# The delta rule's inverse in 32x32 blocks on four strips of partitions, with a step's tail spread over the next step

## The chip, the cores and the metric

One core of one Trainium2 chip runs the whole kernel. The metric is the time of one execution in microseconds (us). The core has TensorE (PE: matrix products into PSUM, with PEld as its weight loads), VectorE (DVE), ScalarE (ACT), GpSimd (POOL) and the DMA queues, of which SyncE (SP) issues most. The engines run side by side, each through its own instructions in order, and wait for each other by semaphores.

## The reference

Two transformer-like blocks run after each other. The change touches one piece of the second: the gated delta rule of its even mixer, run forwards and backwards over 512 + 256 tokens with 8 heads of 64.

```python
m = jnp.where(strict, einsum('bhncd,bhnsd->bhncs', kb, kc) * decay, 0.0)
tmat = triangular_solve(m + eye, eye, left_side=True, lower=True, unit_diagonal=True)
u = einsum('bhncs,bhnsv->bhncv', tmat, vb)
w = einsum('bhncs,bhnsk->bhnck', tmat, kb * exp(gc)[..., None])
qk = einsum('bhncd,bhnsd->bhncs', qc, kc) * decay
def step(s, inp):
    v_new = u_i - einsum('bhck,bhkv->bhcv', w_i, s)
    o_i = einsum('bhck,bhkv->bhcv', qd_i, s) + einsum('bhcs,bhsv->bhcv', qk_i, v_new)
    s = s * gl_i[..., None, None] + einsum('bhck,bhcv->bhkv', kd_i, v_new)
```

`tmat` is the inverse of a unit triangular matrix. It is what the change computes in another way.

## The kernel before

The kernel works in fp32 and in chunks of 128 tokens, so there are 6 token tiles and 2 directions: 12 steps. `order` lists them as (direction, tile), the directions taking turns. In step n all 8 heads lie side by side along the columns of a tile.

A step goes like this. `act_rows` fetches the rows of cumulated gates by a DMA on ACT's queue. `dve_dif` takes differences and clamps them, `act_decays` turns them into decays `DU` and `DD`. `pe_kq` makes the products of keys with keys (which = 0) and keys with queries (which = 1), and `dve_kq` with `dve_kq_rest` multiplies the first into `DU` (the matrix M) and the second into `DD`. `pool_blocks` copies the two 64x64 diagonal blocks of M (8 heads) into `MC`, on partitions 0 to 63 and 64 to 127.

The inverse of these blocks is built by doubling. `XC` holds the inverse so far, `XTC` its transpose. `dve_first` sets the first level (pairs of rows), `pe_xt` transposes it on PE, `act_xt` copies that out. Then come levels 1 to 5. In each, `pool_level` masks out of `MC` the off-diagonal part `Cc` of that level, and `pe_level` computes v = Cc' XTC (16 matmuls of 64x64), which ACT copies to `VC` in two halves (`act_level`), and then z (32 matmuls), which DVE subtracts from `XTC` and `XC`, again in halves (`dve_level`). The last level joins 32x32 blocks to 64x64. Below these two blocks lies one 64x64 corner: `pe_cross`, a copy by ACT, `pe_corner`, a negated copy by DVE (`dve_corner`). `pool_gdn` copies the diagonal blocks into the full 128x128 transposed inverse `XT`.

`pe_state` applies the running state `S` to keys and queries, `pe_u` applies `XT` to the values less the state's part, `pe_s` updates the state, and `pe_o` makes the output. Of step n - 1, `pe_u`, `pe_o` and `pe_s` stand in step n, after its levels 1 and 2. `pe_side` puts other work into the loop: a chunk of a modulation product with 4 MB of weights (line 583) in steps 1, 3, 5, 7 and 9, and its fold (line 569) a step later.

The order on each engine is written out by hand in `pe_gdn`, `act_gdn`, `dve_gdn` and `pool_gdn`. PSUM has 8 banks, given out in turn by `K.open`: a matmul into a bank waits until the reader of its last content is through. Names in rows: `psum` is any bank; `feat`, `weights`, `rows` and `arena` are large tiles in which `XC`, `XTC`, `VC`, `MC`, `XT` and `DU` are columns. The level matmuls are line 2392, cross 2422, corner 2431, kq 2384, state 2444, u 2456, o 2464, s 2473. Short names such as v, z, kq, u in the text are these blocks.

## Time and profile before

| what | us |
|---|---|
| three runs | 3333.03, 3338.39, 3343.77 |
| median | 3338.39 |
| span of the profiled execution | 3342.8 |
| delta rule's loop of 12 steps (1396.3 to 1756.0) | 359.7 |
| its tail (1756.0 to 1768.4) | 12.4 |

The profile gives for the profiled execution its span, from first to last instruction, and no time of its own beside that; it lies among the three runs. PE is busy 94% of the span, DVE 50%, ACT 36%, POOL 9%. A group's row gives line, engine, operation, names and shapes, then how often, busy time, mean length in ns and the idle time ahead of it with what ended it. One fp32 matmul of the program stands as two records in the trace, each with its weight load. In a timeline, records of one kind that follow each other are one row.

### The profile page before, as it was taken

How to read it: one execution, taken by the hardware profiler on the slowest of the kernel's cores; microseconds unless marked ns; L12 is line 12 of the kernel's file. 1: busy time of each engine (PE TensorE's matmuls, PEld its weight loads, DVE VectorE, ACT ScalarE, POOL GpSimd, SP SyncE). 2: the span in 40 equal slices, each digit the busy share in tenths (PEclk: the TensorE clock that was granted, in tenths of full speed). 3: DMA queues.
4: the chain of work that ended last, by engine and by line, in shares of the span. 5: the costliest groups of instructions: out<-in, count | busy, mean ns of one | idle time of the engine just before them, and what ended most of it. 6: DMA issues, size and time to landing. Idle time of an engine off the chain costs nothing.

```text
span 3342.8 us, 55088 instructions
## 1 busy us (share of the span) xinstructions
PE 3137.0 (94%) x23594; PEld 2546.5 (76%) x23594; DVE 1659.0 (50%) x2675; ACT 1194.1 (36%) x2162; POOL 308.1 (9%) x312
## 2 busy tenths in 40 slices
PE   7989998999998999899998899999999988989998
PEld 5767887757776787788885578888888776678886
DVE  3255445344525546776765555333344456653444
ACT  4315335355531554422224444111112425642221
POOL 1020020000002100143431000000000101000000
PEclk9999999989999999999998999999999999999999
DMA  5293212260227331132211003212121324032231
GB/s 212 76 328 104 101 59 101 101 252 26 88 96 265 90 105 54 54 121 72 82 60 42 26 14 81 71 51 76 51 76 51 100 51 76 4 99 78 99 114 64
DMA packets 176062, 306.58 MB, mean 92 GB/s; under 512 B 20326, under 2 KB 41639, under 8 KB 175561
## 3 DMA queue, kind: packets, MB, share of 16 engines
q1 hardware_dynamic: 148064, 278.71, 24.9%
q0 software_dynamic: 3712, 12.74, 1.3%
q10 hardware_dynamic: 24041, 11.60, 1.3%
q8 instruction: 186, 3.05, 0.4%
q14 instruction: 59, 0.48, 0.1%
HBM read 294.87 MB, written 6.80 MB: 90 GB/s over the span
## 4 chain that ended last, share of the span: by engine, by line
PE 71%; DVE 16%; ACT 8%; DMA 2%; issue 1%; POOL 1%; ACTq 0%; DVEq 0%; SPq 0%
PE psum L425 17%; PE psum L426 17%; PE psum L427 17%; PE psum L2392 5%; PE psum L958 3%; PE psum L583 2%; ACT feat L692 2%; PE psum L977 2%; DVE small L1122 2%; DVE weights_r L369 2%; DVE arena L875 1%; DVE x_lat L878 1%; PE psum L992 1%; PE psum L2384 1%; PE psum L2456 1%
## 5 line engine op out<-in xcount | busy, mean ns | idle before, releaser
L369 DVE TENSOR_TENSOR weights_r<-weights,weights_r 128x2048 fp32r<-128x2048 f32 (+2 forms) x168 | 361.5, 2172 | 506.6 <-ACT weights_r L360 506.5
L425 PE MATMUL psum<-feat_r,weights_r 128*128 128x512 f32 (+1 forms) x1552 | 544.2, 351 | 8.5 <-DVE feat_r L722 4.9
L426 PE MATMUL psum<-feat_r,weights_r 128*128 128x512 f32 (+1 forms) x1552 | 541.9, 349 | 0.0
L427 PE MATMUL psum<-feat_r,weights_r 128*128 128x512 f32 (+1 forms) x1552 | 541.1, 349 | 0.0
L425 PE MATMUL psum<-weights_r,feat_r 128*128 128x512 f32 (+2 forms) x1344 | 527.1, 392 | 14.6 <-DVE weights_r L369 10.1
L360 ACT ACTIVATE weights_r<-weights 128x2048 fp32r<-128x2048 f32 (+2 forms) x168 | 303.1, 1825 | 634.4 <-DMA weights<-in_w_ffn_gate 208.2
L427 PE MATMUL psum<-weights_r,feat_r 128*128 128x512 f32 (+2 forms) x1344 | 520.3, 387 | 0.0
L426 PE MATMUL psum<-weights_r,feat_r 128*128 128x512 f32 (+2 forms) x1344 | 520.1, 387 | 0.0
L425 PEld LDWEIGHTS psum<-feat_r,weights_r 128*128 128x128 f32 x1552 | 295.0, 190 | 54.8 <-issue 6.2
L426 PEld LDWEIGHTS psum<-feat_r,weights_r 128*128 128x128 f32 x1552 | 295.1, 190 | 37.6
L427 PEld LDWEIGHTS psum<-feat_r,weights_r 128*128 128x128 f32 x1552 | 294.7, 190 | 37.9
L425 PEld LDWEIGHTS psum<-weights_r,feat_r 128*128 128x128 f32 x1344 | 255.7, 190 | 66.8 <-DVE weights_r L369 10.3
L427 PEld LDWEIGHTS psum<-weights_r,feat_r 128*128 128x128 f32 x1344 | 255.2, 190 | 50.3
L426 PEld LDWEIGHTS psum<-weights_r,feat_r 128*128 128x128 f32 x1344 | 255.8, 190 | 47.9
L425 PE MATMUL psum<-weights_r,arena_r 128*128 128x512 f32 x440 | 172.5, 392 | 5.7 <-DVE arena_r L521 2.8
L426 PE MATMUL psum<-weights_r,arena_r 128*128 128x512 f32 x440 | 171.4, 389 | 0.0
L427 PE MATMUL psum<-weights_r,arena_r 128*128 128x512 f32 x440 | 171.2, 389 | 0.0
L1122 DVE TENSOR_REDUCE small<-psum 128x1 f32<-128x768 f32 (+4 forms) x176 | 121.7, 691 | 42.4 <-PE psum L958 31.0
L700 POOL CAST feat_r<-feat 128x512 fp32r<-128x512 f32 x76 | 51.0, 671 | 864.6 <-ACT feat L692 864.4
L1057 ACT ACTIVATE feat<-psum,small 128x768 f32<-128x768 f32 (+2 forms) x112 | 87.3, 779 | 106.3 <-DVE small L1122 98.8
L977 PE MATMUL psum<-const,feat 128*128 128x128 f32 x544 | 84.3, 286 | 35.6 <-DVE arena L1131 16.7
L692 ACT ACTIVATE feat<-psum,small 128x128 f32<-128x128 f32 x304 | 109.4, 481 | 6.4 <-PE psum L661 6.4
(478 smaller groups left out, 4411.2 us busy)
## 6 DMA issues: line engine op xcount, KB each, us to landing
weights<-in_w_mod SPq DMA_DIRECT2D x48, 2048.0 KB, 13.0
weights<-in_gla_w_in SPq DMA_DIRECT2D x24, 1024.0 KB, 7.3
weights<-in_w_ffn_gate SPq DMA_DIRECT2D x20, 1024.0 KB, 7.6
weights<-in_w_ffn_up SPq DMA_DIRECT2D x20, 1024.0 KB, 5.1
weights<-in_w_ffn_down SPq DMA_DIRECT2D x20, 1024.0 KB, 6.3
weights<-in_fox_w_in SPq DMA_DIRECT2D x16, 1024.0 KB, 6.2
weights<-in_sgu_w_in SPq DMA_DIRECT2D x12, 1024.0 KB, 6.7
weights<-in_gla_w_out SPq DMA_DIRECT2D x8, 1024.0 KB, 6.9
```

The lines of the kernel that those rows point to most:

```text
L360: act.e.activation(WEI_r[:, s * SLOT + HALF:s * SLOT + HALF + n], WEI_t[:, s * SLOT:s * SLOT + n], ACT.Copy).then_inc(*A.put(("weights", c ...
L369: dve.e.tensor_tensor(WEI_r[:, s * SLOT:s * SLOT + n], WEI_t[:, s * SLOT:s * SLOT + n], WEI_r[:, s * SLOT + HALF:s * SLOT + HALF + n].bitc ...
L425: pe.e.matmul(ps, lh, rh, start=first, stop=False)
L426: pe.e.matmul(ps, lh, rl, start=False, stop=False)
L427: done = pe.e.matmul(ps, ll, rh, start=False, stop=last)
L583: done = pe.e.matmul(ps[32 * j:32 * j + 32, :], cond_at(mod, k, b), where[k][0], start=b == 0 and k < 4, stop=b == 1 and k >= 4)
L692: act.e.activation(FL_plain[:, k, t * P:(t + 1) * P], K.at[at][:, m * P:(m + 1) * P], ACT.Identity, bias=PRE_B[:, c0 + k:c0 + k + 1], scal ...
L958: done = pe.e.matmul(ps[m][:, n0:n0 + w], lt, rh, start=first, stop=last)
L977: done = pe.e.transpose(ps[:, c0:c0 + P], PR[n % 3][:, j * P:(j + 1) * P], ident)
L1057: act.e.activation(PR[i][:, 0:nk], src, ACT.Exp, bias=NEGM[:, i:i + 1], accum_out=SUM[:, n % 8:n % 8 + 1]).then_inc(*A.put((tag, "exp", n) ...
L1122: dve.e.tensor_reduce(NEGM[:, i:i + 1], src, AX.X, ALU.max, negate=True).then_inc(*V.put((tag, "max", n)))
L2392: done = pe.e.matmul(out_[rows, (h - heads[0]) * 64:(h - heads[0] + 1) * 64], lhsT[rows, h, :], rhs[rows] if len(rhs.shape) == 2 else rhs[ ...
```

## The change

The inverse by doubling now works on 32x32 diagonal blocks only: four of them per head, one on each strip of 32 partitions (`STRIPS`), so that a head takes 32 columns instead of 64. `XX` holds the transpose and the inverse side by side, `Cc`, `VC` and `MC` have half their columns. There are four levels instead of five. A level has 32 matmuls of 32x32 in v and 64 in z. z's two products of a half go into one bank, and DVE subtracts both in one instruction.

The fifth level becomes a join: `pe_join_v` takes the off-diagonal 32x32 blocks straight from M, ACT copies, `pe_join_z` gives the blocks for `XT` and for `XN` (the inverse of one half, needed by corner), and ACT copies them out negated, in three pieces. The corner's copy moves from DVE to ACT. `pe_xt` and `act_xt` are gone; DVE transposes 32x32 blocks itself in `dve_first`.

The join, cross, corner, u, s and o of step n - 1 are dealt out one by one between the v and z blocks of step n. So are both kq products; the one for queries moves to the end of its own step. `DU` gets a third buffer, since M is needed longer, and its rows are fetched earlier in the step; the semaphore of that DMA becomes two. The decays: DVE clamps only `DD`, in one instruction that also adds a mask of -1e30 (`NEG`), and ACT clamps `DU` by a Relu ahead of its exponential, in an own place. Key products, beta and decay are multiplied in one pass of eight 128x128 instructions (`dve_kk`). POOL copies four blocks, masks three or four levels of half the width, and assembles `XT` and `XN` in six copies (`pool_assemble`). The constant tile grows by 192 columns, and POOL makes the 32-wide identity `IDENT_S` by four small copies ahead of the mixer.

```diff
+    def pe_strips(pe, out_, lhsT, rhs, name=None):
+        for h in range(4):
+            for rows in STRIPS:
+                done = pe.e.matmul(out_[rows, h * 32:(h + 1) * 32], lhsT[rows, h, :], rhs[rows, h, :], start=True, stop=True)
+        if name is not None:
+            done.then_inc(*B.put(name))
+    def pe_v(pe, n, level):
+        C = b2(h8(Cc[level % 2]))
         for hb in range(2):
             at = (D_, "v", n, level, hb)
             ps = K.open(pe, at)
             pe.wait_ge(*G.of((D_, "C", n, level)))
-            pe.wait_ge(*(A if level == 1 else V).of((D_, "x level", n, level - 1, hb)))
-            pe_blocks(pe, ps, h8(C), h8(Xt), range(4 * hb, 4 * hb + 4), at)
+            pe.wait_ge(*V.of((D_, "x level", n, level - 1, hb)))
+            pe_strips(pe, ps, C[:, hb], XX[n % 2][:, 0, 4 * hb:4 * hb + 4, :], at)
+    def pe_z(pe, n, level):
         for hb in range(2):
+            at, v, x = (D_, "z", n, level, hb), b2(h8(VC))[:, hb], XX[n % 2][:, 1, 4 * hb:4 * hb + 4, :]
+            ps = K.open(pe, at)
             pe.wait_ge(*A.of((D_, "v", n, level, hb)))
-            for l_, r_, which in ((X, VC, "xt"), (VC, X, "x")):
-                at = (D_, "z", n, level, hb, which)
-                ps = K.open(pe, at)
-                pe_blocks(pe, ps, h8(l_), h8(r_), range(4 * hb, 4 * hb + 4), at, x_halves(n, level, which))
+            pe_strips(pe, ps, x, v)
+            pe_strips(pe, ps[:, 128:256], v, x, at)
+    def pe_join_v(pe, n):
+        at = (D_, "join v", n)
+        ps = K.open(pe, at)
+        for hb in range(2):
+            pe.wait_ge(*V.of((D_, "x level", n, 4, hb)))
+        for h in range(8):
+            for a in range(2):
+                near, far = strips_of(n, a)
+                done = pe.e.matmul(ps[near, h * 32:(h + 1) * 32], h8(DU[n % 3])[far, h, near],
+                                   XX[n % 2][far, 0, h, :], start=True, stop=True)
+        done.then_inc(*B.put(at))
+    def pe_join_z(pe, n):
+        at = (D_, "join z", n)
+        ps, v = K.open(pe, at), h8(VX[:, 0:256])
+        pe.wait_ge(*A.of((D_, "join v", n)))
+        for h in range(8):
+            x = XX[n % 2][:, 1, h, :]
+            for a in range(2):
+                near, far = strips_of(n, a)
+                done = pe.e.matmul(ps[near, h * 32:(h + 1) * 32], x[near], v[near, h, :], start=True, stop=True)
+                if a == near_half(n):
+                    done = pe.e.matmul(ps[far, h * 32:(h + 1) * 32], v[near, h, :], x[near], start=True, stop=True)
+        done.then_inc(*B.put(at))
...
+        pe.wait_ge(*A.of((D_, "join z", n, "far")))
+        pe.wait_ge(*G.of((D_, "XT far", n)))
...
-        pe_kq(pe, 0, 1)
-        pe_xt(pe, 0)
         for n in range(STEPS):
             more, behind = n + 1 < STEPS, n > 0
-            pe_level(pe, n, 1)
+            pe_v(pe, n, 1)
+            if behind:
+                pe_join_v(pe, n - 1)
+            if more and not from_dram(n + 1):
+                pe_decay(pe, n + 1)
+            pe_z(pe, n, 1)
+            if behind:
+                pe_join_z(pe, n - 1)
+            pe_v(pe, n, 2)
+            if behind:
+                pe_cross(pe, n - 1)
+            pe_z(pe, n, 2)
+            if behind:
+                pe_corner(pe, n - 1)
+            pe_v(pe, n, 3)
+            if more:
+                pe_kq(pe, n + 1, 0)
+            pe_z(pe, n, 3)
             if behind:
                 pe_u(pe, n - 1)
-            if more and not from_dram(n + 1):
-                pe_decay(pe, n + 1)
-            pe_level(pe, n, 2)
+            pe_v(pe, n, 4)
+            if behind:
+                pe_s(pe, n - 1)
+            pe_z(pe, n, 4)
             if behind:
                 pe_o(pe, n - 1)
-                pe_s(pe, n - 1)
-            if more:
-                pe_kq(pe, n + 1, 0)
-            pe_level(pe, n, 3)
             pe_state(pe, n)
-            pe_level(pe, n, 4)
-            pe_level(pe, n, 5)
+            pe_kq(pe, n, 1)
             pe_side(pe, gdn_side(n))
-            pe_cross(pe, n)
-            if more:
-                pe_kq(pe, n + 1, 1)
-                pe_xt(pe, n + 1)
-            pe_corner(pe, n)
+        pe_join_v(pe, STEPS - 1)
+        pe_join_z(pe, STEPS - 1)
+        pe_cross(pe, STEPS - 1)
+        pe_corner(pe, STEPS - 1)
         pe_u(pe, STEPS - 1)
...
+    def act_decay_u(act, n):
         act.wait_ge(*V.of((D_, "clamped", n)))
-        act.e.activation(DU[n % 2], DU[n % 2], ACT.Exp, scale=-1.0).then_inc(*A.put())
-        act.e.activation(DD[n % 3], DD[n % 3], ACT.Exp).then_inc(*A.put((D_, "decays", n)))
+        act.e.activation(DU[n % 3], DU[n % 3], ACT.Relu).then_inc(*A.put())
+        act.chain()
+        act.e.activation(DU[n % 3], DU[n % 3], ACT.Exp, scale=-1.0).then_inc(*A.put((D_, "decays u", n)))
+    def act_decay_d(act, n):
+        act.wait_ge(*V.of((D_, "clamped", n)))
+        act.e.activation(DD[n % 3], DD[n % 3], ACT.Exp).then_inc(*A.put((D_, "decays d", n)))
...
+    def act_join_z(act, n):
+        at, X, a = (D_, "join z", n), h8(XT[order[n][0]]), near_half(n)
+        ps = h8(K.at[at][:, 0:256])
+        act.wait_ge(*B.of(at))
+        act.wait_ge(*G.of((D_, "zeros")))
+        if n >= 2:
+            act.wait_ge(*B.of((D_, "u", n - 2)))
+        near, far = strips_of(n, 1 - a)
+        act.e.activation(X[near, :, far], ps[near], ACT.Copy, scale=-1.0).then_inc(*A.put((*at, "far")))
+        near, far = strips_of(n, a)
+        columns = slice(near.start % 64, near.start % 64 + 32)
+        act.e.activation(h8(XN)[far, :, columns], ps[far], ACT.Copy, scale=-1.0).then_inc(*A.put())
+        act.e.activation(X[near, :, far], ps[near], ACT.Copy, scale=-1.0).then_inc(*A.put(K.frees(A, at), at))
...
+    def dve_clamp(dve, n):
         if n >= 3:
             dve.wait_ge(*B.of((D_, "o", n - 3)))
         dve.chain()
-        dve.e.tensor_scalar(DD[n % 3], dif, 0.0, None, ALU.min).then_inc(*V.put())
-        dve.chain()
-        dve.e.tensor_scalar(dif, dif, 0.0, None, ALU.max).then_inc(*V.put((D_, "clamped", n)))
...
+    def dve_kk(dve, n):
         d, t = order[n]
-        mine = h8((DU[n % 2], DD[n % 3])[which])
+        M = h8(DU[n % 3])
+        dve.wait_ge(*A.of((D_, "decays u", n)))
+        dve.wait_ge(*B.of((D_, "kq", n, 0, 1)))
         for par in range(2):
-            at = (D_, "kq", n, which, par)
-            dve.wait_ge(*B.of((D_, "kq", n, which, 1)))
-            dve.wait_ge(*A.of((D_, "decays", n)))
+            at = (D_, "kq", n, 0, par)
+            for h in range(par, 8, 2):
+                dve.e.scalar_tensor_tensor(M[:, h, :], K.at[at][:, h // 2 * P:(h // 2 + 1) * P],
+                                           BETA[:, t, d * 8 + h:d * 8 + h + 1], M[:, h, :], ALU.mult,
+                                           ALU.mult).then_inc(*V.put(K.frees(V, at), (D_, "m", n)))
...
+        Xt, X = XX[n % 2][:, 0], XX[n % 2][:, 1]
+        dve.e.scalar_tensor_tensor(X, h8(MC), -1.0, rows_over(LEVEL_S[order[n][0]][0], 8), ALU.mult, ALU.mult).then_inc(
             *V.put((D_, "MC read", n)))
         dve.chain()
-        dve.e.tensor_tensor(X, X, rows_over(IDENT_C, 8), ALU.add).then_inc(*V.put((D_, "x", n)))
+        dve.e.tensor_tensor(X, X, rows_over(IDENT_S, 8), ALU.add).then_inc(*V.put())
+        dve.chain()
+        dve.e.transpose(flat(Xt), flat(X)).then_inc(*V.put((D_, "x level", n, 0, 0), (D_, "x level", n, 0, 1)))
     def dve_level(dve, n, level):
         for hb in range(2):
-            half = slice(hb * 256, (hb + 1) * 256)
-            dve.wait_ge(*B.of((D_, "z", n, level, hb, "x")))
+            at, x = (D_, "z", n, level, hb), XX[n % 2].rearrange("p w (b h) c -> p b w (h c)", b=2)[:, hb]
+            dve.wait_ge(*B.of(at))
             dve.chain()
-            for dst, which in ((XTC[n % 2], "xt"), (XC[n % 2], "x")):
-                at = (D_, "z", n, level, hb, which)
-                some = x_halves(n, level, which)
-                rows = slice(some[0].start, some[-1].stop)
-                dve.e.tensor_tensor(dst[rows, half], dst[rows, half], K.at[at][rows, 0:256],
-                                    ALU.subtract).then_inc(*V.put(K.frees(V, at)))
-            V.mark((D_, "x level", n, level, hb))
-    def dve_corner(dve, n):
-        near, far = near_far(n)
-        at = (D_, "corner", n)
-        dve.wait_ge(*B.of(at))
-        dve.e.tensor_scalar(h8(XT[order[n][0]])[near, :, far], h8(K.at[at])[near], -1.0, None,
-                            ALU.mult).then_inc(*V.put(K.frees(V, at), at))
+            dve.e.tensor_tensor(x, x, grid(K.at[at][:, 0:256], 2), ALU.subtract).then_inc(
+                *V.put(K.frees(V, at), (D_, "x level", n, level, hb)))
...
-        dve_kq(dve, 0, 0)
-        dve_kq_rest(dve, 0, 0)
-        dve_kq(dve, 0, 1)
+        dve_clamp(dve, 0)
+        dve_kk(dve, 0)
         dve_first(dve, 0)
-        dve_kq_rest(dve, 0, 1)
         for n in range(STEPS):
             more, behind = n + 1 < STEPS, n > 0
             dve_level(dve, n, 1)
             if more:
                 dve_dif(dve, n + 1)
             dve_level(dve, n, 2)
+            if more:
+                dve_clamp(dve, n + 1)
+            dve_level(dve, n, 3)
+            if more:
+                dve_kk(dve, n + 1)
+            dve_level(dve, n, 4)
             if behind:
                 dve_s(dve, n - 1)
-                dve_o(dve, n - 1)
-            if more:
-                dve_kq(dve, n + 1, 0)
-            dve_level(dve, n, 3)
-            if more:
-                dve_kq_rest(dve, n + 1, 0)
-            dve_state(dve, n)
-            dve_level(dve, n, 4)
             if more:
                 dve_first(dve, n + 1)
-            dve_level(dve, n, 5)
+            if behind:
+                dve_o(dve, n - 1)
+            dve_state(dve, n)
+            dve_qk(dve, n)
             dve_side(dve, gdn_side(n))
-            if more:
-                dve_kq(dve, n + 1, 1)
-                dve_kq_rest(dve, n + 1, 1)
-            dve_corner(dve, n)
         dve_o(dve, STEPS - 1)
...
+    def pool_assemble(pool, n):
+        X, a = h8(XT[order[n][0]]), near_half(n)
+        for hb in range(2):
+            pool.wait_ge(*V.of((D_, "x level", n, 4, hb)))
+        if n >= 2:
+            pool.wait_ge(*B.of((D_, "u", n - 2)))
+        pool.chain()
+        for rows in STRIPS[2 * (1 - a):2 * (1 - a) + 2]:
+            pool.e.tensor_copy(X[rows, :, rows], XX[n % 2][rows, 0]).then_inc(*G.put((D_, "XT far", n)))
+        for s, rows in enumerate(STRIPS[2 * a:2 * a + 2]):
+            pool.e.tensor_copy(h8(XN)[rows, :, 32 * s:32 * s + 32], XX[n % 2][rows, 1]).then_inc(*G.put((D_, "XN", n)))
+        pool.chain()
+        for rows in STRIPS[2 * a:2 * a + 2]:
+            pool.e.tensor_copy(X[rows, :, rows], XX[n % 2][rows, 0]).then_inc(*G.put((D_, "XT", n)))
...
```

On ACT, `act_gdn` follows the same order: level 1, the join's five copies, level 2, cross, the DMA of rows, corner, level 3, the decay of `DU`, u, level 4, the decay of `DD`, and the side row.

PE in a step without a decay product, before: from u of the last step (L2456) to the key products of the next (L2384). L2392 with x16 is v, four of x8 are z.

```order
L2456 MATMUL psum<-rows 128x64 x8
L2392 MATMUL psum<-weights 64x64 x16
L2392 MATMUL psum<-feat,weights 64x64 x8
L2392 MATMUL psum<-weights,feat 64x64 x8
L2392 MATMUL psum<-feat,weights 64x64 x8
L2392 MATMUL psum<-weights,feat 64x64 x8
L2464 MATMUL psum<-arena,feat 128x64 x8
L2473 MATMUL psum<-arena 64x64 x8
L2384 MATMUL psum<-arena 128x128 x8
```

PE at the same place after: from the second half of z2 to s. L2407 is a strip matmul, with x32 for v and x16 for half of z's halves; L2469 is corner, L2397 kq, L2493 u, L2511 s.

```order
L2407 MATMUL psum<-weights,feat 32x32 x16
L2407 MATMUL psum<-feat,weights 32x32 x16
L2469 MATMUL psum<-feat 64x64 x8
L2407 MATMUL psum<-feat,weights 32x32 x32
L2397 MATMUL psum<-arena 128x128 x8
L2407 MATMUL psum<-weights,feat 32x32 x16
L2407 MATMUL psum<-feat,weights 32x32 x16
L2407 MATMUL psum<-weights,feat 32x32 x16
L2407 MATMUL psum<-feat,weights 32x32 x16
L2493 MATMUL psum<-rows,weights 128x64 x8
L2407 MATMUL psum<-feat,weights 32x32 x32
L2511 MATMUL psum<-arena 64x64 x8
```

Corner, kq, u and s now each have a place of their own between two blocks of the levels.

ACT before, one step: copies of v (L2527), u (L2534), the decays (L2519, L2520), the side row (L598), cross (L2576), the DMA of rows.

```order
L2527 ACTIVATE feat<-psum 128x256 x2
L2534 ACTIVATE arena<-psum 128x512
L2527 ACTIVATE feat<-psum 128x256 x2
L2519 ACTIVATE feat<-feat 128x1024
L2520 ACTIVATE feat<-feat 128x1024
L2527 ACTIVATE feat<-psum 128x256 x6
L598 ACTIVATE side_row<-psum 128x512
L2576 ACTIVATE feat<-psum 64x512
L2552 DMA weights<-decay_sums 128x8x128
```

ACT after: the join (L2589 to L2605) and cross (L2612) and corner (L2618) stand between the copies of v (L2580), ahead of the decays (L2567, L2569, L2573).

```order
L2589 ACTIVATE feat<-psum 32x256 x2
L2601 ACTIVATE rows<-psum 32x8x32
L2604 ACTIVATE feat<-psum 32x8x32
L2605 ACTIVATE rows<-psum 32x8x32
L2580 ACTIVATE weights<-psum 128x128 x2
L2612 ACTIVATE feat<-psum 64x512
L2636 DMA feat<-decay_sums 128x8x128
L2618 ACTIVATE rows<-psum 64x8x64
L2580 ACTIVATE weights<-psum 128x128 x2
L2567 ACTIVATE weights<-weights 128x1024
L2569 ACTIVATE weights<-weights 128x1024
L2625 ACTIVATE arena<-psum 128x512
```

The copies of v for levels 2 and 3 now stand behind copies that belong to the step before.

## Rows read from the trace of the kernel before

**Rows 1.** The profile's page, first line: span and instruction count.

```profile
span 3342.8 us, 55088 instructions
```

**Rows 2.** Windows: stretch, its length, then PE, PEld, DVE, ACT, POOL busy (instructions), clock, DMA.

```profile
1396.30:1756.00 359.70, 344.49 (x7680) 311.79 (x7680) 246.92 (x466) 90.80 (x180) 146.16 (x134) 0.99 0.23 78
...
1515.40:1544.30 28.90, 28.48 (x650) 26.82 (x650) 21.54 (x43) 7.64 (x16) 11.99 (x11) 1.00 0.08 21
...
1747.20:1750.60 3.40, 3.40 (x70) 3.40 (x68) 0.30 (x2) 0.77 (x2) 2.64 (x2) 0.50 0.00 0
...
1756.00:1768.40 12.40, 10.19 (x64) 9.71 (x65) 0.69 (x1) 1.19 (x2) 1.22 (x2) 0.56 0.01 1
```

**Rows 3.** Timeline of PE in step 3: start, length, work, [idle before it].

```profile
1484.85 2.00 PE L2456 MATMUL psum<-rows 128*128 128x64 f32 x16
...
1486.77 1.15 PE L2392 MATMUL psum<-weights 64*64 64x64 f32 x32
...
1488.01 0.68 PE L2392 MATMUL psum<-feat,weights 64*64 64x64 f32 x16
...
1490.02 2.00 PE L2464 MATMUL psum<-arena,feat 128*128 128x64 f32 x16
...
1491.95 0.69 PE L2473 MATMUL psum<-arena 128*64 128x64 f32 x16
...
1492.56 1.16 PE L2384 MATMUL psum<-arena 64*128 64x128 f32 x16
...
1493.65 1.15 PE L2392 MATMUL psum<-weights 64*64 64x64 f32 x32
...
1496.83 2.00 PE L2444 MATMUL psum<-arena 64*128 64x64 f32 x32
...
1503.32 1.45 PE L2392 MATMUL psum<-weights 64*64 64x64 f32 x32 [1.31 <-DVE weights L2647]
...
1506.57 3.64 PE L583 MATMUL psum<-weights,cond 128*32 128x512 f32 x32
...
1510.14 1.14 PE L2422 MATMUL psum<-weights 64*64 64x64 f32 x16
...
1512.30 1.15 PE L2392 MATMUL psum<-const,feat 64*64 64x64 f32 x32
...
1513.29 1.09 PE L2431 MATMUL psum<-feat,weights 64*64 64x64 f32 x16
```

**Rows 4.** Timeline of PEld at the start of a side chunk.

```profile
1506.56 0.16 PEld L583 LDWEIGHTS psum<-weights,cond 128*32 128x32 f32 x8
```

**Rows 5.** Groups by form, 1390 to 1770 us: count | busy us, mean ns | idle before.

```profile
L2754 POOL TENSOR_TENSOR weights<-feat,const 128x512 f32<-128x512 f32 x60 | 80.7, 1344 | 83.6 <-PE psum L2392 80.5
...
L2520 ACT ACTIVATE feat<-feat 128x1024 f32<-128x1024 f32 x11 | 11.4, 1041 | 0.0
...
L2527 ACT ACTIVATE feat<-psum 128x256 f32<-128x256 f32 x120 | 46.1, 384 | 152.5 <-PE psum L2392 147.4
...
L2647 DVE TENSOR_TENSOR weights<-weights,psum 128x256 f32<-128x256 f32 x108 | 41.2, 418 | 28.8 <-PE psum L2392 27.4
...
L2612 DVE TENSOR_TENSOR feat<-feat,psum 128x512 f32<-128x512 f32 x34 | 21.8, 683 | 38.2 <-PE psum L2384 38.1
...
L2674 DVE TENSOR_TENSOR rows<-rows,arena 128x512 f32<-128x512 f32 x10 | 13.5, 1351 | 1.0
...
L2534 ACT ACTIVATE arena<-psum 128x512 f32<-128x512 f32 x12 | 7.2, 598 | 46.4 <-PE psum L2456 46.4
...
L2590 DVE TENSOR_TENSOR weights<-weights,arena 128x1024 f32<-128x1024 f32 x5 | 6.1, 1219 | 0.0
```

**Rows 6.** Timeline of PE, first level matmuls of step 0.

```profile
1396.29 1.98 PE L2392 MATMUL psum<-feat,weights 64*64 64x64 f32 x32 [0.78 <-ACT feat L2541]
```

**Rows 7.** Timeline of PE in the last step.

```profile
1746.98 1.85 PE L2392 MATMUL psum<-weights 64*64 64x64 f32 x32 [2.73 <-POOL weights L2754]
```

**Rows 8.** DMA queues in the loop: packets, MB, share of 16 engines.

```profile
q8 instruction: 61, 1.00, 1.2%
```

214 lines of the change are left out of this document (112 added, 102 removed).

## The prediction

> **What bounds the kernel now.** I read the windows first, then TensorE's (PE's) order of work in one step, then what the other engines' instructions of that step take. The whole run has a span of 3342.8 us [rows 1]. The delta rule's loop of 12 steps is 359.7 us of it and its tail another 12.4 [rows 2]. In the loop PE is busy 344 of 359.7 us, VectorE (DVE) 247, ScalarE (ACT) 91, GpSimd (POOL) 146. A step without side work is the stretch 1515.4 to 1544.3: 28.9 us, PE 28.5 busy, DVE 21.5 [rows 2]. So PE's queue sets the step, and only what leaves that queue gains.
>
> The queue of one step, from the starts of its blocks [rows 3] (a block's own length ends about 0.07 us after the next may start, so I take differences of starts or lengths less 0.07): u 1.92, o 1.93, s 0.61, kq 1.09 twice, state 1.93, cross 1.07, corner 1.02. Together 10.7 us, which the change keeps. A level (v, the wait for ACT's copy, z) is 1486.77 to 1490.02, 3.25 us. Five of them, half a z less in the last, are 15.7. The transpose xt is 0.99, and PE waits 1.31 us before level 5 for DVE. The sum is 28.7, against 28.9 in the window.
>
> **Part 1: the levels.** The page counts two records for one fp32 matmul. Before, a level has 16 matmuls in v and 32 in z, 96 records. After, the blocks are 32x32: 32 and 64 matmuls, 192 records, but only four levels, so 768 records a step instead of 464. All hangs on what one costs. [rows 3] show 32 v records of 64x64, on two diagonal tiles of the array, in 1.15 us. Less the last one's 0.22 that is 30 ns a record, or 60 on each tile. The corner's 16 records on a single tile take (1.09 - 0.22)/15 = 58 ns each. So two tiles run at once, and a tile's record takes 58 to 60 ns at 64 columns. The kq block, 128 columns on two row halves, gives (1.16 - 0.27)/15 = 59 ns, 118 on each tile. The time of a tile goes with its columns: about 30 ns at 32. Four tiles at once make 7.5 ns a record, if the queue can hand them out that fast. In the side chunk eight weight loads for four column tiles start within 0.16 - 0.11 = 0.05 us, 7 ns apart [rows 4]. That is a short burst from a full queue; no row shows it kept up. I take 8 ns, since both rows are nearest to this shape; the other end is 30 ns, the closest spacing that long rows keep up. Then a level is 1.5 us of PE, four are 6.2.
>
> The Trainium skill's page "TensorE: Matmul & The Clock Gate", in the section "Wait — 56ns, not 53.3ns?", speaks against this: it puts a floor of about 25 ns under the distance of two matmul starts, however few columns they have. The trace has starts 7 ns apart on different tiles, so I read the floor as one of a single tile; taken for all tiles it makes a step of 32.5 us and a run of about 3382.
>
> **Part 2: joins for a fifth level.** join_v has 16 matmuls, join_z 24, 80 records. They use two or three tiles at a time, so 15 ns each: 1.2 us. They replace the fifth level, xt and the 1.31 us wait. The transpose goes to DVE as one 128x256 instruction. No row has one; the nearest of that size takes 0.42 us [rows 5], and even at three times that it lies in DVE's slack.
>
> **Part 3: the moved tail.** Of step n-1 the joins, cross, corner, u, s and o now stand one by one between v and z, or between z and the next v, of step n. That is where PE used to wait for ACT. The chain that v waits for is: copy by ACT of 128x128 (384 ns at 256 columns, 598 at 512, so 277 at 128), z, DVE's 128x256 subtraction 0.42 us [rows 5]. With about 0.05 for each handover, z may start 0.8 us after v starts, and the next v 0.2 us after z's last start for one half, 0.75 for the other. Each filler is at least 0.5 us (join_v 0.5, cross 1.07, kq 1.09, s 0.61 ahead of z; join_z 0.7, corner 1.02, u 1.92, and o, state, kq 4.95 ahead of v). So the chain is covered with one exception, next.
>
> The fillers put waits into the in-order queues. On ACT the copies of v2 stand behind join_z's three copies (1.15 us), those of v3 behind corner's, which PE only issues after z2. Both end near the time at which PE has finished cross and kq, so I price them at 0 to 0.3 us; if these fillers were shorter it would be 1 us each. On DVE state and qk are last: 1.37 + 1.35 + 1.37 us [rows 5] behind a PE block that ends when the step ends. They hold the first subtraction of the next step until about 3.2 us into it, where PE wants it at 2.0 to 2.5: 0.7 us late. POOL's work per step (three 128x256 masks and a fourth, 10 copies of 32 rows, the three 128x512 products of 1.2 to 1.5 us) is some 10 us, with its results wanted a quarter of a step later or more; the zeroing of XT and XN costs about 2.6 us once, in step 0.
>
> DVE's own sum: levels 8 x 0.42, dif and clamp 1.22 each, eight 128x128 products at 0.29 (the line through 0.42 and 0.68), s 0.84, first and transpose 1.3, o 0.68, state 2.7, qk 1.4: 15 us. ACT: 2.2 + 1.9 for the joins, 1.2 for cross and corner, 3.1 for three decays (1.04 each [rows 5]), u 0.6: 9 us. Neither sets a step of 20.
>
> **The step after:** 6.2 + 1.2 + 10.7 = 18.0 on PE. About ten more changes of tile shape at 0.07 us each make 18.7, DVE's lateness 0.7 makes 19.4. The last term is the fetch of instructions. [rows 8] have 61 packets of 1.00 MB in the loop, for 15360 PE records and loads and some 780 others: 62 bytes each. They took 1.2% of 16 x 359.7 us, 1.13 us for one of 16 KB, 4.3 ns an instruction and 8.6 ns a record with its load. That is just the strips' rate. I add 1.1 us a step for stretches where it doesn't keep up: 20.5.
>
> **The sum.** Twelve steps save 12 x (28.9 - 20.5) = 101 us. Step 0 has no tail of an earlier step and saves some 4 more. The five side chunks (3.6 us of PE each [rows 3]) stay, but part of what they covered is gone: -3. The tail after the loop was 12.4 us at a granted clock of 0.56 [rows 2]; it gets two joins and their copies in series, 4.5 us. Ahead of the loop xt, its copy and one pair of products fall away before the first level, which began at 1396.3 [rows 6]: 3 us sooner. The weights' loads and the decay rows are issued no later within their step than before. What follows the loop shifts as it is. In all 100 us: 3342.8 - 100 = 3243 against the profiled span. The span lies within the three runs and 4 us above their median, 3338.4, so **3238** against the median.
>
> **Rivals.**
> Rival 1, slower: PE's queue can't hand out 32x32 records faster than the 30 ns of today's long rows. For it: no row shows better over more than eight instructions, and an instruction count that doubles. Against it: today's 30 ns is explained by two tiles at 58 to 60 ns, and [rows 4]. Price: 848 records x 22 ns = 18.7 us a step, less the 1.8 us of waits that this hides: 37.4 a step, 12 x 8.5 = 102 slower, 3440. It decides from 8.4/848 = 10 ns above my 8: at 18 ns a record nothing is gained.
> Rival 2, slower: the clock. The granted clock is 0.99 over the loop and 1.00 in the plain step, falls to 0.50 from 1747.2 on [rows 2], behind a wait of PE of 2.7 us [rows 7], and is 0.56 in the tail. After, PE has shorter work and more small waits. At 1.2 GHz all the way the 18.7 us double: 12 x 8.5 = 102 slower. It needs the low level in 45% of the loop to cost the whole gain. Against it: my step has PE idle for 2 us of 20, never over 1 at a time. A low stretch in step 0 or in the tail is likelier, and costs 2 to 6 us.
> Rival 3, a smaller gain: the in-order queues or the fetch bind. If corner's copy holds v3, the state products hold the next step, and the fetch runs at twice my allowance, 3 to 4 us come back: 24 a step, saving 59, time 3280.
> Rival 4: the change does what it says but nothing moves, because records cost 17 to 19 ns: within 0.3% of before.
>
> **Chances.** Forecast (3205 to 3265) 0.62; rival 3 and other partial gains (3265 to 3328) 0.18; rival 4 0.04; rival 1 with its milder forms 0.11; rival 2 0.05. This kernel's measurement can tell about 0.3%, 10 us, from no change. That gives faster 0.80, same 0.04, slower 0.16. The range must leave out the two slower cases and no more: 3205 to 3330. The low end has step 0, switches and fetch at nothing (19.0 a step).
>
> **What would show it.** Right: L2407 (the strip matmuls) with 32 records of v in 0.45 us or less; a plain step of 19 to 22 us; PE's idle time spread in pieces under 1 us; DVE's level subtraction waiting for PE, not for itself; a clock of 1.00 between the first and last step. Wrong in part 1 if 32 records take 0.8 us or more. Wrong in part 3 if PE waits over 1 us for ACT's copies ahead of z2 or z3, or over 1.5 us for DVE at v2. Wrong in the fetch term if weight loads wait for "issue" within a block. Wrong as a whole if windows in the loop show the clock at 0.5, or if the part behind the loop grows by more than 5 us.

## The result: slower, and the loop at the low clock with waits for instructions

The changed kernel takes 3421.93 us (median of four runs, 3418.71 to 3434.94) against 3339.77 us for the kernel before (four runs too, 3333.03 to 3343.77). The ratio is 1.0249, with a 95% interval of 1.0229 to 1.0269. I had forecast 3238. The profiled execution has a span of 3423.2 us, 80 more than before [rows 1]. One of the four runs of a kernel below, before_split, took 3624.9 us at a lower granted clock, and its time is the median of the other three.

The page of the kernel after, its first line and its row of the granted clock in 40 slices:

```profile
span 3423.2 us, 63434 instructions
...
PEclk9999999999999999665667999999999999999999
```

The low stretch is the delta rule's loop. Windows of the same kernel, with the columns of [rows 2] (length, then PE, PEld, DVE, ACT, POOL busy, clock, DMA share, GB/s): from the first v to the last z, the time from there to the end of the last o, a plain step, and the step ahead of it, which holds a side chunk:

```profile
1384.90:1824.80 439.90, 362.95 (x11809) 322.38 (x11809) 153.03 (x328) 102.24 (x222) 112.27 (x188) 0.63 0.18 60
1824.80:1852.80 28.00, 24.34 (x222) 23.23 (x220) 5.35 (x9) 4.85 (x13) 5.08 (x9) 0.50 0.16 55
1704.50:1740.70 36.20, 28.87 (x1008) 27.05 (x1000) 14.51 (x31) 8.82 (x19) 10.38 (x17) 0.64 0.23 76
1670.60:1704.50 33.90, 29.04 (x1028) 24.65 (x1024) 14.49 (x29) 9.42 (x20) 9.28 (x16) 0.75 0.07 20
```

The loop is 440 us instead of some 360 [rows 2]. Its mean granted clock is 0.63 instead of 0.99, and PE is idle for 77 us of it instead of 15. From corner to corner, a plain step takes 36.2 to 44.2 us (four of them, at clocks of 0.50 to 0.64) where it took 28.9 and where I had forecast 20.5. The five steps with a side chunk take 33.9 to 41.3 us, no longer than the plain ones though they hold more work, at clocks of 0.62 to 0.75. Both of my reasons for a clock of 1.00 and a small fetch term are gone, so the two questions are where the 77 us come from and where the clock goes.

The waits of the same stretch (engine, line, what it waited for, total us, times, longest):

```profile
DVE feat L2738 <- PE psum L2407: 255.7, 94, 7.5
POOL weights L2832 <- PE psum L2407: 136.6, 23, 10.8
ACT weights L2580 <- PE psum L2407: 108.9, 30, 15.8
PEld psum L2407 <- issue: 79.1, 62, 4.2
PE psum L2407 <- issue: 66.7, 45, 4.0
```

DVE, POOL and ACT all wait for the strip matmuls (L2407). Those wait for "issue", that is for nothing that any semaphore shows. With the other lines' pieces it is 74.8 us; before it was 0.4 us in the loop.

PE's timeline of the kernel after, in steps 8 and 9 (start, length, work, [idle before]):

```profile
1714.42 0.58 PE L2407 MATMUL psum<-feat,weights 32*32 32x32 f32 x25 [2.31 <-issue]
1714.93 3.67 PE L2493 MATMUL psum<-rows,weights 128*128 128x64 f32 x16
1718.53 1.08 PE L2407 MATMUL psum<-feat,weights 32*32 32x32 f32 x64
1719.54 1.12 PE L2511 MATMUL psum<-arena 128*64 128x64 f32 x16
...
1724.69 2.00 PE L2481 MATMUL psum<-arena 64*128 64x64 f32 x32
1726.52 1.11 PE L2397 MATMUL psum<-arena 64*128 64x128 f32 x16
1727.57 1.05 PE L570 MATMUL psum<-const,side_row 128*128 128x4 f32 x8
1728.55 0.74 PE L2407 MATMUL psum<-feat,weights 32*32 32x32 f32 x63
1729.11 0.21 PE L2436 MATMUL psum<-feat,weights 32*32 32x32 f32 x1
...
1736.50 0.53 PE L2407 MATMUL psum<-feat,weights 32*32 32x32 f32 x21 [2.45 <-issue]
```

Three things stand here. At full clock the 64 records of a v take 1729.11 - 1728.55 = 0.56 us, 8.8 ns each: the strips run as fast as forecast. At half clock the same block takes 1719.54 - 1718.53 = 1.01 us, 15.8 ns, and u takes 3.6 us instead of 1.92 [rows 3]. And a block of v or z that was running stops in its middle for 2.3 us.

PE's instructions come by DMA, in packets of 16 KB. The instruction queue's own row in this window (packets, MB, share of 16 engines) answers to [rows 8]:

```profile
q8 instruction: 92, 1.51, 1.4%
```

92 packets in 440 us, one for every 257 of the window's 23618 matmul records and loads: a packet holds 256. Their start times in the trace are never less than 3.27 us apart, with a median of 3.91; one takes about 1.0 us to transfer (median; 1.09 on the mean). My reading is that a stop comes when PE has used up the 256 instructions (128 matmul records and 128 loads) of a packet and the next is not there yet; strips_twice below bears it out.

### The profile page after: what moved, and what is told of

It is laid out like the page before. It is cut to its first block, busy times and chain, and to the rows that moved or that the text cites. A ratio compares the mean times of both kernels' runs of the same rounds, so it can differ in the third digit from the quotient of the medians.

```text
span 3423.2 us, 63434 instructions
## 1 busy us (share of the span) xinstructions
PE 3154.4 (92%) x27818; PEld 2557.4 (75%) x27818; DVE 1567.7 (46%) x2543; ACT 1207.7 (35%) x2210; POOL 277.4 (8%) x377
## 4 chain that ended last, share of the span: by engine, by line
PE 72%; DVE 14%; ACT 8%; issue 4%; DMA 1%; POOL 0%; ACTq 0%; DVEq 0%; SPq 0%; POOLq 0%
PE psum L426 16%; PE psum L428 16%; PE psum L427 16%; PE psum L2407 4%; PE psum L959 3%; PE psum L584 3%; PE psum L978 2%; DVE small L1123 2%; ACT feat L693 2%; DVE weights_r L370 2%; DVE arena L876 1%; PE psum L2397 1%; PE psum L2501 1%; PE psum L2493 1%; DVE x_lat L879 1%
## 5 line engine op out<-in xcount | busy, mean ns | idle before, releaser
L2407 PE MATMUL psum<-feat,weights 32*32 32x32 f32 x6144 | 113.4, 223 | 49.7 <-issue 46.9
L2738 DVE TENSOR_TENSOR feat<-feat,psum 128x256 f32<-128x256 f32 x96 | 40.5, 421 | 256.8 <-PE psum L2407 256.6
L1123 DVE TENSOR_REDUCE small<-psum 128x1 f32<-128x768 f32 (+4 forms) x176 | 121.6, 691 | 41.2 <-PE psum L959 29.8
L2407 PEld LDWEIGHTS psum<-feat,weights 32*32 32x32 f32 x6144 | 94.9, 135 | 60.3 <-issue 53.7
```

The lines of the kernel that those rows point to most:

```text
L1123: dve.e.tensor_reduce(NEGM[:, i:i + 1], src, AX.X, ALU.max, negate=True).then_inc(*V.put((tag, "max", n)))
L2407: done = pe.e.matmul(out_[rows, h * 32:(h + 1) * 32], lhsT[rows, h, :], rhs[rows, h, :], start=True, stop=True)
```

## The experiments

In the table the loop is the stretch from the first to the last matmul of v or z (in before and before_split it begins with the transpose xt, 2 us ahead of the first v), its clock is from the windows, the wait for issue from the waits of PE, and the distance of packets from their start times. A ratio is to runs of the kernel before in the same session.

| kernel | time, us | ratio (95%) | loop, us | clock | wait for issue, us | median distance, us |
|---|---|---|---|---|---|---|
| before | 3340 to 3344 | 1 | 360.5 | 0.99 | 0.4 | 5.58 |
| after | 3421.9 | 1.0249 (1.0229 to 1.0269) | 439.9 | 0.63 | 74.8 | 3.91 |
| wide_strips | 3397.5 | 1.0157 (1.0140 to 1.0174) | 411.8 | 0.92 | 50.9 | 3.89 |
| strips_twice | 3714.4 | 1.1105 (1.1088 to 1.1121) | 721.4 | 0.59 | 203.8 | 3.77 |
| tail_gathered | 3426.0 | 1.0244 (1.0227 to 1.0261) | 446.3 | 0.64 | 57.1 | 4.20 |
| before_split | 3582.7 | 1.0713 (1.0672 to 1.0753) | 587.4 | 0.85 | 9.4 | 4.72 |
| one_z | 3340.6 | 0.9987 (0.9969 to 1.0006) | 338.7 | 0.67 | 30.0 | 4.25 |
| one_z_64_columns | 3319.2 | 0.9937 (0.9919 to 0.9955) | 342.2 | 0.78 | 33.9 | 4.25 |
| one_z_wide | 3307.6 | 0.9894 (0.9876 to 0.9912) | 319.9 | 0.94 | 29.8 | 4.03 |
| one_z_filler | 3330.6 | 0.9968 (0.9955 to 0.9981) | 346.7 | 0.92 | 21.5 | 4.51 |
| v_on_64 | 3389.1 | 1.0133 (1.0109 to 1.0156) | 402.2 | 0.55 | 1.8 | 6.42 |
| v_64_by_64 | 3328.7 | 0.9958 (0.9941 to 0.9975) | 341.4 | 0.72 | 14.5 | 5.60 |
| v_on_64_wide_z | 3316.2 | 0.9902 (0.9869 to 0.9935) | 323.2 | 0.87 | 7.9 | 5.44 |

The first strips start between 1384.9 and 1392.6 us of the span from kernel to kernel, so loops compare to within some 7 us. one_z scattered more than the others: 3324.57 to 3352.58 in ten runs.

My first theory (F) was that the supply of instructions makes PE idle, and that the clock falls behind this idle time. The rivals were the clock by itself (C), the chain of copies (L) and slow starts of small matmuls (P).

### Wider streams through the same strips

```diff
-done = pe.e.matmul(out_[rows, h * 32:(h + 1) * 32], lhsT[rows, h, :], rhs[rows, h, :], start=True, stop=True)
+done = pe.e.matmul(out_[rows, h * 32:128], lhsT[rows, h, :], rhs[rows, h:4, :], start=True, stop=True)
```

> The changed kernel with only one edit: each strip matmul of v and z for head h of a half streams the columns of heads h to 3 (128, 96, 64 or 32 columns instead of 32) and writes as many; the surplus columns are overwritten by the later heads' own matmuls, so results are the same. The number of PE instructions is the same, their work in the array is 2.5 times as large (some 19 ns a record by the widths, instead of 8 to 9). Theory F (instruction supply, with the clock behind it): the changed kernel's loop is bound by a fetch of one 16 KB packet of 256 instructions at a time, at best one per 3.3 to 3.4 us (13 ns an instruction, 27 ns a strip record), PE idles 1 to 4 us at the packets' borders, and the granted clock falls behind these idle times. Then 2.5 times the array work is free: the wait for issue in the loop drops from 67 us below 30, the granted clock of the loop rises from 0.62 to 0.85 or more, a plain step takes 28 to 32 us instead of 37, and the time is 3310 to 3370, below the changed kernel's 3422. Theory C (the clock alone: PE falls to 1.2 GHz because work on 32x32 tiles counts little, and there it is just slow): the clock stays near 0.6 and the added columns cost 768 x 10 ns x 1.6 = 12 us a step: 3500 to 3570. Theory P (the small matmuls themselves are slow to start): no gain either, 3420 or more.

Measured: 3397.5 us, 24 less than the changed kernel, with the same instructions and 2.5 times as many streamed columns in the strips. The loop's window of wide_strips:

```profile
1392.10:1803.90 411.80, 358.17 (x11809) 325.39 (x11809) 149.82 (x328) 102.50 (x223) 111.35 (x188) 0.92 0.19 64
```

and the largest of PE's waits in it:

```profile
PE psum L2407 <- issue: 45.3, 36, 3.3
```

The clock came back to 0.92, as F said and C did not. But the wait for issue fell only to 50.9 us and not below 30, and the time missed F's range by 27 us. A high clock with 36 waits of up to 3.3 us in front of L2407 is already a poor fit to "the clock falls behind idle times".

### Half of z by a transpose on DVE, narrow and wide

```diff
-            pe_strips(pe, ps, x, v)
-            pe_strips(pe, ps[:, 128:256], v, x, at)
+            pe_strips(pe, ps, x, v, at)
...
-            dve.e.tensor_tensor(x, x, grid(K.at[at][:, 0:256], 2), ALU.subtract).then_inc(
-                *V.put(K.frees(V, at), (D_, "x level", n, level, hb)))
+            dve.e.tensor_tensor(x[:, 0], x[:, 0], K.at[at][:, 0:128], ALU.subtract).then_inc(*V.put(K.frees(V, at)))
+            dve.chain()
+            dve.e.transpose(x[:, 1], x[:, 0]).then_inc(*V.put((D_, "x level", n, level, hb)))
```

> The changed kernel with half of z left to DVE: of the two products of z only the one for the transpose is made on PE (32x32 blocks), DVE subtracts it (128x128 instead of 128x256) and then transposes the 32x32 blocks into the inverse, which is the same value. Strip records per step fall from 768 to 512, PE's instructions from about 2000 to 1490 (5.8 packets of 256). DVE gets 8 transposes of 128x128 a step, about 0.3 us each, and 8 subtractions shrink by 0.14 us. Theory F (fetch floor of 3.4 us a packet): a step is bounded at 5.8 x 3.4 = 20 us, and with packets that hold long matmuls taking longer 22 to 26 us; the time is 3220 to 3300 if the clock stays up, up to 3350 if gaps of 1 us are still enough to bring it down. Theory C (small tiles bring the clock down whatever the supply): the clock stays near 0.6, PE's work of 16 us a step becomes 32, time 3370 to 3400. Theory L (what costs is the serial chain of ACT's copies and DVE's subtraction): DVE's chain per half is longer by 0.15 us, so 3422 or more.

The second kernel adds the diff of wide_strips to this one.

> Both edits together: one product of z a level, and strip matmuls that stream 128, 96, 64 and 32 columns. 512 strip records of some 19 ns make the array's work about 21.6 us a step, against a fetch of 5.8 packets x 3.4 = 20 us. Theory F: PE hardly runs dry any more; wait for issue in the loop below 15 us, clock 0.9 or more, step 23 to 26 us, time 3250 to 3300; about equal to the version with one product alone if that one's clock stays up, and faster than it if its clock falls. Theory C: clock near 0.6, 512 x 10 x 1.6 = 8 us a step more than with one product alone: some 3450 or more.

Measured: 3340.6 and 3307.6 us. The loop's window of one_z, narrow:

```profile
1392.60:1731.30 338.70, 304.01 (x8737) 269.75 (x8737) 171.10 (x423) 102.13 (x222) 113.91 (x188) 0.67 0.22 76
```

and of one_z_wide:

```profile
1392.60:1712.50 319.90, 288.05 (x8737) 259.46 (x8737) 171.12 (x423) 102.14 (x222) 112.36 (x188) 0.94 0.24 80
```

The largest of PE's waits in one_z:

```profile
PE psum L2407 <- issue: 23.6, 17, 2.8
```

and in one_z_wide:

```profile
PE psum L2407 <- issue: 22.3, 22, 2.9
```

A quarter fewer PE instructions take 81 us off the changed kernel: the loop is 101 us shorter, of which 59 us are PE's busy time, and the wait for issue is 30 us instead of 75. So the number of instructions is one cause of the waits. C's 3370 to 3400 for one_z is out, and F's forecast holds only in its milder form (up to 3350 if the clock falls). For one_z_wide F missed: it wanted a wait for issue below 15 us and at most 3300. The pair then refutes the second half of F. Both have the same instructions, the same wait for issue (30.0 and 29.8 us) and nearly the same idle time (35 and 32 us), yet the narrow one has a clock of 0.67 and the wide one 0.94. DVE's longer chain (L) costs nothing that shows. I formed a new theory, C2: it is the narrow streams that go with the low clock, with or without waits.

### The kernel before, with its 64 columns in two halves

```diff
-            for rows in halves:
-                done = pe.e.matmul(out_[rows, at:at + 64], lhsT[rows, h, :], rhs[rows, h, :], start=True, stop=True)
+            for c in (0, 32):
+                for rows in halves:
+                    done = pe.e.matmul(out_[rows, at + c:at + c + 32], lhsT[rows, h, :], rhs[rows, h, c:c + 32], ...)
```

> The kernel before with only one edit: each level matmul of 64x64 with 64 columns is written as two of 32 columns. The array's work is the same (60 ns a record on a tile at 64 columns, 30 at 32), the order, the tiles and the other engines are the same; level records per step rise from 464 to 928, PE's instructions from about 1230 to 2150. Theory F: a packet of 256 instructions holds 128 level records, 1.9 us of array work, and the next one arrives only 3.4 us after; so PE waits for issue inside the levels, the loop's steps grow from 28.9 to 32 to 37 us, with a clock that may fall behind the gaps: 3380 to 3450. Theories C and L, and the view that 32x32 tiles are the trouble: no 32x32 tile and no new chain here, the clock stays at 0.99 and the time within 0.3% of 3338.

Measured: 3582.7 us, far above every expectation, and not for F's reason: the wait for issue is 9.4 us. The array itself took twice as long. PE's timeline of before_split at full clock:

```profile
1576.71 2.06 PE L2398 MATMUL psum<-weights 64*64 64x32 f32 x64
1578.60 1.10 PE L2398 MATMUL psum<-feat,weights 64*64 64x32 f32 x32
1579.54 1.10 PE L2398 MATMUL psum<-weights,feat 64*64 64x32 f32 x32
```

64 records with 32 columns take 1.89 us, 29.5 ns each, as much as those with 64 columns before (30 ns, [rows 3]). So at this shape the time is not set by the streamed columns. What sets it is the 64 columns of weights that each record loads, 59 ns on each of two tiles. [rows 3] already had the counterpart: state (L2444) has the 64 rows and the 64 streamed columns of v but 128 columns of weights, also on two tiles, and its 32 records take 1.93 us, 60 ns each and 120 on a tile, twice v's 60. The Trainium skill's page "TensorE: Matmul & The Clock Gate", section "LDWEIGHTS (loading the stationary operand)", says that a load takes a time in proportion to the weights' columns, whatever their rows; its formula gives an estimate of 53 ns for 64. The 59 ns of this run lie near it. F is not tested by it as meant: 128 records at 29.5 ns are 3.8 us a packet, more than the least distance of packets, so hardly any wait was to be had. The clock fell from 0.99 to 0.85 with the streamed columns halved.

### Supply without the waits: v on 64x64 tiles

POOL writes the masked block C into the diagonal blocks of 64x64 tiles that are zero elsewhere, so that one matmul does two strips of v. In z the strips stay.

```diff
+            for h in range(4):
+                for rows in (lo_, hi_):
+                    done = pe.e.matmul(ps[rows, h * 32:(h + 1) * 32], h8(C64)[rows, 4 * hb + h, :],
+                                       XX[n % 2][rows, 0, 4 * hb + h, :], start=True, stop=True)
...
+        for s, rows in enumerate(STRIPS):
+            pool.e.tensor_tensor(h8(C64)[rows, :, 32 * (s % 2):32 * (s % 2) + 32], h8(MC)[rows],
+                                 rows_over(LEVEL_S[order[n][0]][level][rows], 8), ALU.mult).then_inc(...)
```

> One product of z a level (as in the run before), and v in half as many matmuls: POOL writes the masked block into the diagonal 32x32 blocks of 64x64 tiles that are zero elsewhere (four instructions of 32 partitions, one buffer of 512 columns in place of two of 256), so one matmul with 64x64 weights and 32 columns does two strips. The results are the same. Strip and level records a step: 256 in z and 128 in v, all PE instructions about 1230 a step, as few as in the kernel before: 4.8 packets, 16.4 us at the floor of 3.4 us. The runs so far show 30 ns a record for 64x64 weights on two tiles with 32 columns as with 64, and 8.5 ns for 32x32 weights with 32 columns, so the array's work is 4 x (0.96 + 0.54) + 1.2 + 10.7 = 18 us. Theory F (supply): wait for issue in the loop under 12 us; at a clock of 0.9 or more a step of 21 us and 3240 to 3275. Theory C2 (the clock falls with narrow columns on 32x32 tiles, whether or not PE waits for instructions: it was 0.67 with one z and narrow columns, 0.92 with wide ones, at nearly the same idle time): half of the strips' time is now the 64x64 form; the clock comes out between, 0.75 to 0.9, and the time 3270 to 3300.

Measured: 3389.1 us, 48 more than one_z though it has fewer instructions. By the 8.5 and 30 ns a record of its expectation it has some 20 us more array work at full clock (256 x 8.5 + 128 x 30 ns a step against 512 x 8.5), but its loop is 63 us longer. The loop's window of v_on_64:

```profile
1392.30:1794.50 402.20, 380.41 (x7201) 344.51 (x7201) 171.67 (x423) 102.12 (x222) 221.83 (x330) 0.55 0.18 62
```

the two largest waits for issue in it:

```profile
PE psum L2419 <- issue: 1.0, 4, 0.3
PE psum L2452 <- issue: 0.6, 1, 0.6
```

and a stretch of PE's timeline:

```profile
1537.20 2.08 PE L2397 MATMUL psum<-arena 64*128 64x128 f32 x16
1539.21 1.07 PE L2407 MATMUL psum<-weights,feat 32*32 32x32 f32 x64
1540.21 3.67 PE L2495 MATMUL psum<-rows,weights 128*128 128x64 f32 x16
1543.82 1.92 PE L2419 MATMUL psum<-feat,weights 64*64 64x32 f32 x32
1545.67 1.12 PE L2513 MATMUL psum<-arena 128*64 128x64 f32 x16
```

This is the sharpest reading of the study. PE is busy for 380 of 402 us, it waits 1.8 us for issue, in the stretch shown its blocks follow each other without a gap, and the clock is 0.55: u takes 3.6 us instead of 1.92. The low clock is no consequence of the supply. Both ranges for the time were missed, F's (3240 to 3275) and C2's (3270 to 3300), and C2's clock of 0.75 to 0.9 was too high.

When the clock was high in this kernel shows in three windows around a side chunk (L584 here), and in PE's timeline there:

```profile
1457.20:1521.90 64.70, 63.81 (x1064) 59.11 (x1068) 28.73 (x70) 15.19 (x31) 34.55 (x54) 0.50 0.24 83
1522.00:1528.70 6.70, 5.17 (x200) 3.17 (x192) 2.29 (x5) 2.94 (x8) 3.11 (x4) 1.00 0.02 5
1528.90:1593.60 64.70, 63.71 (x1060) 59.04 (x1064) 29.27 (x71) 15.19 (x31) 34.85 (x54) 0.50 0.25 83
...
1519.27 4.95 PE L584 MATMUL psum<-weights,cond 128*32 128x512 f32 x32
```

In the first and third window PE is busy for 99% of the time at the low clock. The clock rises in the middle of the side chunk, whose matmuls stream 512 columns, and is low again soon behind it. It is the same at the other four side chunks, and nowhere else after the start of the loop does it leave the low level. The Trainium skill's page "TensorE: Matmul & The Clock Gate", in its section "What's actually happening", ties the clock to how busy PE was of late and calls the low state that of an idle engine. Here the engine was busy for 95% of the loop by the profile and still had the low clock (1.2 GHz) for most of it, so that busy share did not keep the clock up. The other 20 us of idle time are waits of up to 3.2 us for DVE and POOL; that they bring the clock down is the rival that the next kernel settles.

One edit on top, and another:

```diff
-                    done = pe.e.matmul(ps[rows, h * 32:(h + 1) * 32], h8(C64)[rows, 4 * hb + h, :],
-                                       XX[n % 2][rows, 0, 4 * hb + h, :], start=True, stop=True)
+                    done = pe.e.matmul(ps[rows, h * 32:to * 32], h8(C64)[rows, 4 * hb + h, :],
+                                       XX[n % 2][rows, 0, 4 * hb + h:4 * hb + to, :], start=True, stop=True)
```

with `to = min(h + 2, 4)`.

> The kernel with v on 64x64 tiles and narrow z, in which PE waited only 1 us for issue in the whole loop and yet had a clock of 0.55. One edit: three of four v matmuls stream 64 columns instead of 32. In the split kernel a 64x64 record cost 30 ns on two tiles at 32 columns and at 64 alike, so at an equal clock this costs nothing, and z, supply and order are the same. Theory C2: the clock rises to 0.75 or more and the loop shrinks from 399 us to 330 to 360: time 3305 to 3350. If what counts is only how often the array stands still, or the 32x32 tiles as such, nothing changes: 3380 to 3395, clock 0.55.

The other leaves v as it is and gives z the wide streams of the first diff.

> The same, and z's strip matmuls stream 128, 96, 64 and 32 columns (19 ns a record). The array's work is 4 x (0.96 + 1.25) + 1.2 + 10.7 = 20.7 us a step, the supply 16.4. Theory C2: clock 0.95 or more, a step of 22 to 23 us, 3255 to 3285, less than or equal to the same kernel with narrow columns. If the clock is all that widening buys and the narrow version's clock holds anyway, the wide one is slower by up to 2.8 us a step, some 30 us.

Measured: 3328.7 and 3316.2 us. The first streams twice the columns in three quarters of v's matmuls, at no array time (before_split). Its loop:

```profile
1388.40:1729.80 341.40, 307.88 (x7201) 279.67 (x7201) 173.62 (x423) 102.13 (x222) 222.89 (x330) 0.72 0.21 73
```

Useless columns alone, with the same instructions and order, raised the clock from 0.55 to 0.72 and took 61 us off the loop and 60 off the kernel, though PE's idle time rose from 22 to 34 us. Time and loop are in C2's ranges, the clock just below its 0.75. The second has 0.87 and missed its range by 31 us. POOL's four pieces of a mask take 3.1 to 4.2 us there, and v of level 2 starts only behind them: PE stood 2.05 and 1.25 us before it in the two steps around 1505 and 1531, which the profile puts down to DVE, though the mask ended last. In the loop PE waits 26 us for POOL and DVE against 8 for issue. That is probably why it doesn't beat one_z_wide.

### Useless work elsewhere, and 64 columns

```diff
-            pe_strips(pe, ps, x, v, at)
+            pe_strips(pe, ps, x, v)
+            pe.e.matmul(ps[:, 128:512], ident, CONST[:, 0:384], start=True, stop=True).then_inc(*B.put(at))
```

> The kernel with one z product and narrow strips, with one useless 128x128 matmul of 384 columns behind each half of z (8 a step, into unused columns of z's bank; nothing reads them). By kq's rate (59 ns for 128 columns on one of two row halves) each costs 0.65 us, together 5.2 us of array work a step for 32 instructions, 1/8 packet. The strips themselves are untouched. Theory C2, any streamed columns count: the clock rises from 0.67 to 0.9 or more, and since part of the filler lies where PE would wait for the next packet, the time is 3290 to 3325, below the 3340 of the same kernel without it, though it does more work. If only the strips' own narrowness mattered, the clock stays near 0.67 and the filler costs 5.2 to 8 us a step: 3400 or more.

Measured: 3330.6 us with 96 useless matmuls added (five runs, 3323.79 to 3335.63); one_z's median is 10 us higher, but its ten runs scatter over all of that range, so a gain is not shown. The loop's window of one_z_filler:

```profile
1385.90:1732.60 346.70, 323.19 (x8927) 239.28 (x8927) 169.84 (x423) 102.13 (x222) 112.53 (x188) 0.92 0.22 74
```

and the group of the useless matmuls in it (two records each; count, busy us, mean ns):

```profile
L2426 PE MATMUL psum<-const 128*128 128x384 f32 x191 | 97.2, 593 | 0.0
```

The loop of the profiled run is 8 us longer than one_z's, so the useless work did not shorten it. But PE was busy with it for 97 us, and the clock of 0.92 instead of 0.67 paid for nearly all of that: the time is far from the 3400 that was expected if only the strips' own narrowness mattered. It missed C2's range by 6 us at the upper end. The columns need not be in the strips.

> The kernel with one z product, its strip matmuls streaming the columns of two heads (64, and 32 for the last) instead of one head's 32 or the 128, 96, 64, 32 of the wide form. Results and instruction count are the same as with one z. Array time by the widths: 13.5 ns a record, between 8.5 and 19.5; 512 of them 6.9 us a step instead of 4.4 or 10. Theory C2 (the granted clock follows the columns that stream, not the idle time): the loop's clock lies between 0.67 and 0.94, near 0.85, and the time between 3300 and 3325. If the clock is already at 0.94 with 64 columns, the array's 3 us a step less than the wide form show only where no packet is waited for: 3290 to 3305.

Measured: 3319.2 us and a clock of 0.78, between narrow (0.67) and wide (0.94), as C2 said. The time is in its range.

### Doubling the strips, and the third part undone

```diff
-            for rows in STRIPS:
+            for rows in STRIPS + STRIPS:
```

> The changed kernel with every strip matmul of v and z issued twice; the second writes the same values. This doubles the disputed cost and nothing else: 768 records more a step, 1536 instructions, 6 packets. Theory F (supply, 3.4 us a packet, 27 ns a record): 6 x 3.4 = 20.5 us a step more, 12 steps 245 us, time 3640 to 3700. If a record cost only its array time at the clock seen in the loop (8.5 ns at 2.4 GHz, 17 at 1.2): 6.5 to 13 us a step, time 3500 to 3580. Rate of v and z within a packet unchanged.

Measured: 3714.4 us, 14 above F's range and 134 above that of array time alone. 9216 more records made the loop 281.5 us longer, 30.5 ns a record, where within a packet they take 9 to 16. That is F's side of it, 3.9 us a packet for the 72 packets more; 153 us of it are busy time and 128 idle. Two stops in PE's timeline of strips_twice:

```profile
1565.98 0.38 PE L2407 MATMUL psum<-feat,weights 32*32 32x32 f32 x12 [1.14 <-issue]
1566.16 0.24 PE L2407 MATMUL psum<-weights,feat 32*32 32x32 f32 x1
1566.16 0.25 PE L2407 MATMUL psum<-feat,weights 32*32 32x32 f32 x3
1566.21 1.00 PE L2407 MATMUL psum<-weights,feat 32*32 32x32 f32 x60
1567.01 0.24 PE L2407 MATMUL psum<-feat,weights 32*32 32x32 f32 x1
1567.02 0.25 PE L2407 MATMUL psum<-weights,feat 32*32 32x32 f32 x3
1567.07 0.84 PE L2407 MATMUL psum<-feat,weights 32*32 32x32 f32 x47
1569.82 0.42 PE L2407 MATMUL psum<-feat,weights 32*32 32x32 f32 x14 [1.91 <-issue]
```

Between the ends of the two stops lie 127 records (128 with one that the trace lacks, 256 instructions with the loads) and 3.84 us. They run in 1.93 us and PE waits 1.91.

The last kernel keeps strips and joins and undoes the dealing out of the tail (here PE's order; ACT, DVE and POOL follow it):

```diff
             pe_v(pe, n, 1)
-            if behind:
-                pe_join_v(pe, n - 1)
...
             pe_z(pe, n, 1)
+            if behind:
+                pe_u(pe, n - 1)
...
             pe_z(pe, n, 4)
+            pe_side(pe, gdn_side(n))
+            pe_join_v(pe, n)
+            pe_kq(pe, n, 1)
+            pe_join_z(pe, n)
+            pe_cross(pe, n)
+            pe_corner(pe, n)
```

> The changed kernel with the third part undone: the strips and the joins stay, but each step does its levels with v and z next to each other, then the side chunk, its joins, cross and corner in a row, with the key products between them; u, o, s of the last step stand after levels 1 and 2, state after level 3, as in the kernel before. Records and instructions are the same. Theory F: supply is bound by packets whatever the order, and because only one packet is ahead, long runs of strips get nothing from the long blocks elsewhere: 6.6 packets of strips and joins x 3.4 = 22.5 us and 10.7 us of the rest, 33 at full clock, and DVE's and ACT's chain is hidden by the waits for instructions; with the clock as low as in the changed kernel 38 to 42 us a step, 3420 to 3480. If dealing out the tail was itself the harm (in-order queues behind it), undoing it gives less than 3400. If dealing out is what hides the chain of copies, each level loses about 1.3 us here: 3480 to 3500.

Measured: 3426.0 us, the same as the changed kernel within 0.1%. PE waits less for issue (57.1 us) and 7.5 us in front of L2469 and some 5 in front of L2459 for ACT. The time is in F's range (3420 to 3480) and in neither of the other two. In the changed kernel the third part is worth nothing that shows, and does no harm either, perhaps because the waits for instructions hide what it would hide. What it is worth without them was not tried.

## Why the prediction was wrong, point by point

- **What bounds the kernel before** (PE's queue, 28.7 us a step): nothing speaks against it. What it left out is that 256 instructions of the levels last 3.8 us there, against packets that come at best some 3.3 us apart. The kernel before stood close to this limit (its own closest packets are 3.27 us apart) and waited 0.4 us in the whole loop.
- **Part 1, 8 ns a record:** right in the number, 8.8 ns at full clock. The step behind it was wrong: "the time of a tile goes with its columns", by which I meant streamed columns. before_split shows that at 64x64 it is the columns of the weights, and the prediction had the row that told so (state, 1.93 us). For 32x32 blocks both shrink, so the number survived by luck. The floor of 25 ns that the Trainium skill's page "TensorE: Matmul & The Clock Gate" gives in "Wait — 56ns, not 53.3ns?" does not hold across tiles, as the prediction had read it; its evidence then was a row of weight loads, not of matmuls, and only the 8.8 ns measured here are about matmul starts. Its 3382 us came nearer than my 3238, but by another mechanism.
- **Part 2 and DVE's transpose:** as forecast in size. The 128x256 transpose takes 0.45 us in the trace of after.
- **Part 3:** no wait of over 1 us for ACT's copies and none over 1.5 us for DVE in a plain step, but this says little, since the waits for instructions lie over them. tail_gathered shows no gain from it.
- **The fetch term, 1.1 us a step:** the first step that failed. I took the 1.13 us that a packet takes [rows 8] as the price of a packet. Its transfer takes as long after, 1.09 us on the mean, but the next one starts 3.3 us after it at the earliest and 3.9 in the median. So 256 instructions cost 3.3 us or more, 13 ns each, not 4.3. The measured wait is 74.8 / 12 = 6.2 us a step. The sign I had named, weight loads that wait for "issue" within a block, is there 62 times.
- **The clock:** the second step that failed, and the larger one in busy time. Rival 2 had the low clock and what it takes to lose the gain by it (the low level in 45% of the loop), at a chance of 0.05, but put it down to shorter work and small waits. A mean of 0.63 between the levels 1 and 0.5 is the low one for (1 - 0.63)/0.5 = 74% of the loop. I had argued from idle time, "PE idle for 2 us of 20, never over 1 at a time". v_on_64 and v_64_by_64 show that this is not what decides: 22 us of idle time, 1.8 of it for issue, and a clock of 0.55; 34 us, and 0.72. Wider streams brought the clock back in each of the five kernels that had them.
- **The sizes:** my sum had 12 x 18.7 + 18 = 242 us of PE work in the loop and 12 x (0.7 + 1.1) = 22 us of idle time. The trace has 363 busy and 77 idle. So 121 us more are busy and 55 more idle, nearly all of it for issue; a loop of 264 became one of 440. The clock accounts for the busy part: by an estimate, if the 363 us were spread evenly over both levels, 74% of them at half rate cost 0.74 x 363 / 2 = 134 us. Each alone is enough to lose the gain: v_on_64 with hardly a wait for issue has a loop of 402 us, wide_strips with a clock of 0.92 one of 412 (some of each is the kernel's own: masks and larger tiles in the first, wider streams in the second).
- **Rival 1** (30 ns a record because the queue hands out no faster) gave 3440 and was closest to the time. Its price is what strips_twice measured, 30.5 ns. That it came close is luck, since it is not a rate of starts: within a packet records start 9 to 16 ns apart.
- **Head and tail:** the first strips start 11 us before [rows 6] (4 to 11 from kernel to kernel), more than the 3 forecast, and then wait 2.7 and 4.0 us for issue. Behind the loop the last step's joins, cross, corner, u and o run at a clock of 0.50 throughout and take 28.0 us; before, cross, corner, u and o took 13.5 from the same point. That is 14.5 us more where 4.5 were forecast, and one of the named signs of a prediction wrong as a whole (over 5).

What stays open: what of the narrow streams the clock responds to, why packets do not follow each other faster than some 3.3 us (no run changed it), and how the loss divides at full clock without added work, which was not tried.

one_z_wide beats both kernels: 3307.6 us, ratio 0.9894 to before. It keeps the change, leaves half of z to DVE's transpose, and streams more columns than it needs.

## What to carry to other kernels

Before you replace large matmuls by more small ones, count TensorE's instructions over the stretch and divide by the time: here a stretch ran dry when 256 instructions were done in less than the 3.3 to 3.9 us between packets. A packet's transfer time is not its distance to the next; the latter is seen only where the queue is hard pressed, so a kernel that shows no wait says nothing of the margin. Then ask how many columns stream in that time, since a TensorE that the profile calls 95% busy with narrow matmuls can run at 1.2 GHz, and all its large matmuls with it; streaming spare columns can be worth more than it costs.

## What was unexpected of the hardware

- The granted clock was 0.55 in a loop with PE busy for 95% of it and 1.8 us of waits for instructions, and 0.94 in one with 30 us of such waits. Between kernels with the same instructions it went 0.67, 0.78, 0.94 with strips that stream 32, 64 and up to 128 columns.
- Instruction packets of 16 KB for PE never started less than 3.25 us apart in the loops of the thirteen kernels, with medians of 3.8 to 3.9 us where PE ran dry most, though one took only about 1 us.
- A 64x64 fp32 record took 29.5 ns on two tiles with 32 streamed columns and 30 with 64, while 32x32 records on four tiles took 8.8 ns.
- 97 us of useless matmuls cost a kernel nothing: the clock of the loop was 0.92 with them and 0.67 without.
- In v_on_64 the clock left its low level five times after the start of the loop, each time in the middle of a side chunk, which streams 512 columns.
